# Two blocks on one core: the seam from the last feed-forward panel to the second block's first panel, met tile by tile

## The reference

```
block 1: x += mixed(rmsnorm(x) @ w_in) @ w_o            # differential attention and retention
         x += cross_attention(rmsnorm(x), rmsnorm(mem)) @ w_xo
         x += (silu(hf @ w_gate) * (hf @ w_up)) @ w_down,  hf = rmsnorm(x);  D_FF = 5632
         x  = rmsnorm(x) * norm_f_g
block 2: h  = rmsnorm(x) * pre_g * (1 + scale) + shift   # scale, shift from silu(c) @ w_ada + b_ada
         q, k, v, gate_a, u, gate_p = split(h @ w_in_2)
         windowed attention and pooling, gated, merged through w_merge, then w_out, a norm and the residual
```

## Time and profile before

| what | value |
|---|---|
| median of 3 runs | 2111.03 us |
| profiled execution's own time | 2107.38 us |
| its span | 2105.6 us |
| granted TensorE clock, mean | 0.998 |
| PE busy | 2062.9 us (98%) |
| VectorE busy | 1678.6 us (80%) |
| ScalarE busy | 1174.8 us (56%) |
| GpSimd busy | 72.9 us (3%) |
| moved by DMA | 453.75 MB, mean 215 GB/s |

### The profile page before, as it was taken

How to read it: one execution, slowest core, us unless ns; L and a number is a source line. 1 busy time by engine, 2 the same in 40 slices (tenths; PEclk the granted TensorE clock), 3 DMA queues, 4 the chain that set the end, 5 groups by cost and what they waited for, 6 DMA issues and landing times.

```text
span 2105.6 us, 25372 instructions
## 1 busy us (share of the span) xinstructions
PE 2062.9 (98%) x9334; PEld 1697.2 (81%) x9334; DVE 1678.6 (80%) x1839; ACT 1174.8 (56%) x1519; POOL 72.9 (3%) x94
## 2 busy tenths in 40 slices
PE   9999999999999999999999999999899999999998
PEld 7877888788887888888888888888678888888786
DVE  6777778876766788998889888898688768988875
ACT  6665656755554565554555555555556645554453
POOL 1000000000000000000000000000310000000000
PEclk9999999999999999999999999999999999999999
DMA  9555557565543458777777777675465556789752
GB/s 341 162 178 167 179 173 245 198 202 191 187 162 131 160 190 285 251 260 252 237 239 258 259 242 248 234 273 204 131 201 180 180 190 221 269 289 319 230 196 105
DMA packets 218955, 453.75 MB, mean 215 GB/s; under 512 B 14400, under 2 KB 16592, under 8 KB 218704
## 3 DMA queue, kind: packets, MB, share of 16 engines
q1 hardware_dynamic: 212928, 432.07, 61.0%
q0 software_dynamic: 5616, 19.94, 3.0%
q10 hardware_dynamic: 288, 0.13, 0.0%
HBM read 447.88 MB, written 4.19 MB: 215 GB/s over the span
## 4 chain that ended last, share of the span: by engine, by line
PE 83%; issue 7%; DVE 6%; ACT 3%; DMA 1%; POOL 0%; DVEq 0%; ACTq 0%; POOLq 0%
PE ps L1068 26%; PE ps L1070 26%; PE ps L1069 26%; DVE wlo L2311 2%; PE ps L648 2%; ACT whi L1587 1%; PE ps L798 1%; PE ps L778 1%; DVE raw L2324 0%; ACT junk L1099 0%; PE ps L884 0%; PE ps L926 0%; PE ps L915 0%; PE ps L864 0%; DMA FR<-in_mem_dram 0%
## 5 line engine op out<-in xcount | busy, mean ns | idle before, releaser
L2311 DVE TENSOR_TENSOR wlo<-raw,whi 128x1024 fp32r<-128x1024 f32 x832 | 1006.5, 1221 | 261.1 <-ACT whi L1587 255.0
L1587 ACT ACTIVATE whi<-raw 128x1024 fp32r<-128x1024 f32 x840 | 882.4, 1057 | 592.5 <-PE ps L1070 551.4
L1068 PE MATMUL ps<-whi,ah 128*128 128x512 f32 x1618 | 642.9, 397 | 13.6 <-DVE wlo L2311 5.5
L1070 PE MATMUL ps<-whi,al 128*128 128x512 f32 x1618 | 631.6, 390 | 0.0
L1069 PE MATMUL ps<-wlo,ah 128*128 128x512 f32 x1618 | 630.5, 390 | 0.0
L1068 PEld LDWEIGHTS ps<-whi,ah 128*128 128x128 f32 x1618 | 304.2, 188 | 80.1 <-issue 8.3
L1070 PEld LDWEIGHTS ps<-whi,al 128*128 128x128 f32 x1618 | 304.1, 188 | 64.7
L1069 PEld LDWEIGHTS ps<-wlo,ah 128*128 128x128 f32 x1618 | 304.5, 188 | 61.0 <-issue 0.2
L1068 PE MATMUL ps<-whi,bh 128*128 128x512 f32 x862 | 341.2, 396 | 3.5 <-DVE wlo L2311 3.1
L1070 PE MATMUL ps<-whi,bl 128*128 128x512 f32 x862 | 336.1, 390 | 0.0
L1069 PE MATMUL ps<-wlo,bh 128*128 128x512 f32 x862 | 335.6, 389 | 0.0
(11 more groups left out here) (235 smaller groups left out, 1335.6 us busy)
## 6 DMA issues: line engine op xcount, KB each, us to landing
raw<-in_w_in_dram SPq DMA_DIRECT2D x168, 512.0 KB, 4.5
raw<-in_w_ada_dram SPq DMA_DIRECT2D x96, 512.0 KB, 4.6
raw<-in_w_gate_dram SPq DMA_DIRECT2D x88, 512.0 KB, 4.8
raw<-in_w_up_dram SPq DMA_DIRECT2D x88, 512.0 KB, 5.0
raw<-in_w_down_dram SPq DMA_DIRECT2D x88, 512.0 KB, 5.4
raw<-in_w_merge_dram SPq DMA_DIRECT2D x64, 512.0 KB, 4.9
raw<-in_w_o_dram SPq DMA_DIRECT2D x32, 512.0 KB, 4.7
raw<-in_w_xk_dram SPq DMA_DIRECT2D x32, 512.0 KB, 4.6
```

Of the source, the lines that this page charges most:

```text
L1068: e.matmul(o, xh[:, k, tokens], wh, start=first, stop=False, skip_group_check=more)
L1070: ins = e.matmul(o, xl[:, k, tokens], wh, start=False, skip_group_check=more, stop=kk == 1 and (st.end or st.form in READ))
L1587: done(e.activation(whi[:, n % HALVES, :], place(item), ACT.Copy), "hi")
L2311: done(e.tensor_tensor(wlo[:, n % HALVES, :], src, whi[:, n % HALVES, :].bitcast(F32), ALU.subtract), "lo")
```

## The change

- e3 and kv meet six halves tile by tile instead of four: e3 all its six, kv its first six.
- The first two halves of e3 are split into `ah` and `al` (places of chunks 2 and 3), the first two of kv into the buffers of the forms; the ring of 4 goes on with the others. `_slots` works out for every half where it lies, from when that is free, and at which step it is made (for single-tile steps no more than 4, in kv 3, steps ahead of its use).
- The low parts of kv are made by VectorE like all others; GpSimd makes none.
- The pieces alternate between two pairs of banks, T and A, and their order is (0,0), (1,0), (2,0), (0,1), (1,1), (2,1), (3,1), (3,0).
- The work at the end of e3 is cut up: `down_sum`, `down_gain`, `down_mean` on VectorE, `down_square`, `gain_square` on ScalarE; and `modulated` into `mod_sums` and `mod_high` or `mod_low`. A job `second_input` orders them by step. Tile 1's sum comes at the end of e3, ahead of chunk 0's low part for tile 0.

```diff
@@ Stream
-        made = self._done + HALVES
...
+        for h, at in {("e", 3): ((0, ("a", 2)), (1, ("a", 3))),
+                      ("kv", 0): ((0, "forms_a"), (1, "forms_b"))}.get((panel.kind, panel.i), ()):
+            self.aside_at[base + h] = at
+        by_tile = HALVES + sum(base <= m for m in self.aside_at)
+        a, b = {"first": (0, by_tile), "last": (n - by_tile, n), None: (n, n)}[panel.stagger]
...
+    def _slots(self):
+        self.slot, self.slot_free, ring = {}, {}, []
+        for n in range(self.total):
+            if n in self.aside_at:
+                self.slot[n], self.slot_free[n] = self.aside_at[n], self.free[n]
+            else:
+                self.slot[n] = len(ring) % HALVES
+                self.slot_free[n] = ring[-HALVES] + 1 if len(ring) >= HALVES else 0
+                ring.append(n)
...
+        met = made = 0
+        for i, st in enumerate(self.steps):
+            ahead = len(self.steps)
+            if len(st.tiles) == 1 and st.form is None:
+                ahead = 3 if self.panels[st.p].stagger == "first" else HALVES
+            while made < self.total and self.slot_free[made] <= met and (
+                    made in self.aside_at or first_use[made] <= i + ahead):
+                made += 1
+            self.steps[i] = st._replace(made=made)
+            if st.taken:
+                met = st.n + 1
@@ PE
-                    jobs.start(pause(2))
-                    for j, tt in (first_order, second_order)[t]:
-                        jobs.start(modulated(j, tt))
-                    if t == 1:
+                    if t == 0:
+                        jobs.start(pause(4))
+                        for j, tt in mod_order:
+                            jobs.start(modulated(j, tt))
+                            if (j, tt) in ((1, 0), (2, 0)):
+                                jobs.start(pause(1))
+                    else:
                         jobs.start(make_forms())
                         jobs.start(first_result())
@@ ScalarE
+            def second_input():
+                yield from pause(4)
+                mod_sums(0, 0)
+                mod_high(0, 0)
+                yield
+                yield
+                mod_sums(1, 0)
+                gain_square(1)
+                mod_high(1, 0)
+                yield
+                yield
+                scale_chunk(1, 1)
+                mod_sums(2, 0)
+                mod_high(2, 0)
+                yield
+                for i, (j, t) in enumerate(mod_order[3:]):
+                    for nj, nt in mod_order[5 + i:6 + i]:
+                        if nj % 2:
+                            scale_chunk(nj, nt)
+                    mod_sums(j, t)
+                    mod_high(j, t)
+                    yield
@@ VectorE
+            def second_input(p):
+                yield from pause(4)
+                scale_chunk(2, 0)
+                mod_sums(0, 0)
+                yield
+                yield
+                mod_low(0, 0)
+                down_gain(p, 1)
+                mod_sums(1, 0)
+                yield
+                down_mean(1)
+                mod_low(1, 0)
+                yield
+                scale_chunk(0, 1)
+                mod_sums(2, 0)
+                mod_low(2, 0)
+                yield
...
                 elif kind == "e":
-                    last_down(p, t)
+                    down_sum(p, t)
+                    if t == 0:
+                        down_gain(p, t)
+                        down_mean(t)
+                        scale_chunk(0, t)
+                        jobs.start(second_input(p))
+                    else:
+                        jobs.start(make_forms("mod"))
+                        jobs.start(first_result())
@@ make, VectorE
-                    if n in stream.pool_halves:
-                        continue
-                    src = place(stream.entries[n].item)
+                    hi, lo = split_at(n)
                     e.wait_ge(s["hi"], n + 1)
@@ GpSimd
             final_roots(0)
-            low_parts(4)
             final_roots(1)
-            low_parts(8)
```

More of the change, by code:

```diff
@@ L267, in __init__ @@
         self._places()
+        self._slots()
         self._loads()
@@ L287, in _step @@
               aside=None):
-        made = self._done + HALVES
-        self.steps.append(Step(n, p, c, hf, tiles, form, start, end, made, job, taken, snap, aside))
-        if taken:
-            self._done = n + 1
+        self.steps.append(Step(n, p, c, hf, tiles, form, start, end, None, job, taken, snap, aside))
         if end:
@@ L594, in hs_done, with mod_banks @@
         def hs_done(j, t):
-            return s[f"hs{j % 2}"], 2 * (j // 2) + t + 1
+            own = [c for c in mod_order if c[0] % 2 == j % 2]
+            return s[f"hs{j % 2}"], own.index((j, t)) + 1
+        def mod_banks(j, t):
+            return A if mod_order.index((j, t)) % 2 else T
         def tmp_before(j, t):
@@ L611, in hi_lo, with split_at @@
             return [buf[:, 4 * c:4 * c + 4, :] for buf in at[name]]
+        def split_at(n):
+            at_n = stream.slot[n]
+            if isinstance(at_n, int):
+                return whi[:, at_n, :], wlo[:, at_n, :]
+            if isinstance(at_n, tuple):
+                parts = [buf[:, 4 * at_n[1]:4 * at_n[1] + 4, :] for buf in at[at_n[0]]]
+            else:
+                parts = [buf[:, :, :] for buf in forms[at_n[-1]]]
+            return [part.rearrange("p a b -> p (a b)") for part in parts]
         def two(ap, b):
@@ L832, in modulated @@
                 e.wait_ge(*hs_done(j, t))
-                for b in range(2):
-                    take(T[b], f"mod{j}{t}")
+                banks = mod_banks(j, t)
+                for bank in banks:
+                    take(bank, f"mod{j}{t}")
                 for k in range(4):
-                    ins = e.transpose(T[k // 2].ap[:, (k % 2) * P:(k % 2 + 1) * P],
+                    ins = e.transpose(banks[k // 2].ap[:, (k % 2) * P:(k % 2 + 1) * P],
                                       hs_of(j, t)[:, k * P:(k + 1) * P], ident[:, :])
                     if k % 2:
-                        ins.then_inc(T[k // 2].full, 1)
+                        ins.then_inc(banks[k // 2].full, 1)
                 yield
@@ L1608, in scalar_program @@
                     jobs.step()
-                if st.end and panels[st.p].stagger == "last" and i + 1 < len(stream.steps):
+                if st.end and panels[st.p].kind == "out" and panels[st.p].stagger and i + 1 < len(stream.steps):
                     make(stream.steps[i + 1].made)
@@ L2040, in last_down, with mod_sums @@
                 done(e.tensor_scalar(col, col, 1.0 / D, None, ALU.mult), "ms")
[L2041 to L2057, removed]
+            def mod_sums(j, t):
+                tmp, bank, label = tmp_of(j, t), mod_banks(j, t)[1], f"mod{j}{t}"
+                e.wait_ge(bank.full, bank.n(label))
                 before = tmp_before(j, t)
@@ L2359, in pool_program @@
             e.memset(ones[:, :], 1.0).then_inc(s["ones"], 1)
-            made = [0]
             def root(name, of, src, dst):
```

124 lines of the change are left out of this document (58 added, 66 removed).

## The result

| | before | after |
|---|---|---|
| median of 6 runs | 2110.22 us (2108.13 to 2111.13) | 2103.86 us (2102.03 to 2105.48) |
| profiled execution, its span | 2107.38, 2105.6 us | 2103.96, 2102.1 us |
| seam: e3's first matmul to the pair's first normal step | 58.77 us | 53.86 us |

The ratio after to before is 0.9972, 95% interval 0.9960 to 0.9985: 0.28% faster, 3 to 8 us. The forecast was 2106.3, 4.7 us less than the kernel before; the medians of six runs differ by 6.4.

The account below looks back on a forecast made before the run. TensorE, busy 98%, bounds the kernel; only 14.1 us of seam waits can be won. Seam 54.4 against 58.8 gives 4.4 less, with a later 0.3 wait 4.7 less, off 2111.0: 2106.3 us; 8-in-10 range 2100.5 to 2111.0.

Parts of the forecast that it names:

- timetable: Each engine's queue in the seam rebuilt from the new order, e3's first matmul = 0: 54.4 us against 58.8.
- the wait of 0.33 in the pair: Later wait in the pair, at 1550.84 on a low part; should go, 0.3 us, since result products now precede the pair.
- First chunk: kv's first half: PE starts at 20.7 after waiting 3.4 us, the fourth half's low part preceding tile 1's sum.
- Second chunk: kv's third half: PE ready at 23.9, starts at 26.7, a 2.8 us wait behind the fifth half's low part.
- Third chunk: Tile 0's third chunk in kv: PE ready at 29.9, starts at 30.3, a wait of 0.4 us.
- Tile 1's chunks: Tile 1's five chunks in kv: low parts done 32.7 to 41.0, no wait; before, waits cost over 4 us.
- the banks' gain: Second pair of banks lets PE turn a chunk before the last is read; gain counted within tile 1's chunk times.
- End of kv: Seventh half at 45.2 after a 2.1 us wait; pair's third step at 54.4 after waiting 0.9.
- Low parts moved: Eight low parts from GpSimd add 9.8 us to VectorE; 7.5 of stretch returns; its total goes from 41.6 to some 44.
- Rival 1: Cover works better than the queues say: only chains count in the seam, 10 us less, 2101; chance 0.2.
- Rival 2: Gain lost again in the pair through VectorE's queue: 1.7 us less is left, 2109.3; chance 0.22.
- Rival 3: VectorE becomes the bound as the stretch stays: 7.6 us later, 2.9 slower than before, 2113.9; chance 0.08.

Follow-up runs that it names:

- experiment 10: Changed kernel with kv's third and fourth half split one step earlier in e3; seam 53.97 us.
- experiment 6: Changed kernel with tile 1's sum behind chunk 0's low part instead of ahead of it; seam 56.39 us.
- experiment 7: experiment 6's kernel with PE kept busy in its three waits by 13, 9 and 9 matmuls of ones; seam 54.47 us.
- experiment 4: Changed kernel with all eight pieces turned into one pair of banks, T; seam 53.89 us.
- experiment 5: experiment 1's kernel with two pairs of banks, order of the pieces kept; seam 58.87 us.
- experiment 1: Kernel before with only kv's low parts moved from GpSimd to VectorE; seam 58.85 us.
- experiment 11: experiment 10's kernel with kv's fifth and sixth half also split one step later; seam 51.56 us, median 2099.95 us, ratio to before 0.9962.
- experiment 12: experiment 11's kernel with the pair's forms two job steps later; seam 49.41 us, median 2099.98 us, ratio to before 0.9956.
- experiment 9: Changed kernel without halves in idle buffers, four halves by tile for six, pause two steps for four; seam 65.03 us.
- experiment 8: experiment 1's kernel with 12 matmuls of ones ahead of chunk 1's transposes; seam 60.25 us.
- experiment 2: Changed kernel with kv's low parts back on GpSimd; seam 55.84 us.
- experiment 3: experiment 2's kernel with PE kept busy by 14 and 8 matmuls of ones in two waits; seam 55.58 us.

## Why the prediction was right

- **The number.** 2103.86 lies within the range for 8 in 10 (2100.5 to 2111.0) and just under the forecast's own (2104.5 to 2108.0); as a difference, 6.4 us is just inside its 3 to 6.5. The timetable accounts for 5.2 of it (below).
- **Where.** All that could be won was placed in the seam, as 14.1 us of waits. Of the 58.77 us the change took 4.91, and the wait of 0.33 in the pair went as said. From e3's first matmul to the end the profiled executions took 2105.6 - 1481.4 = 624.2 and 2102.1 - 1483.7 = 618.4 us, 5.8 less.
- **First chunk.** Predicted at 20.7, measured 1504.22 - 1483.71 = 20.5. The waiting low part of kv's fourth half in front of the sum is in VectorE's rows and in experiment 10.
- **Second chunk.** Predicted at 26.7, measured 26.2; but the wait was 0.6, not 2.8: PE was late itself, with 8 matmuls at half clock, and that filled the wait. The clock was not in my timetable. It cost nothing here, because what PE lost it would have waited; experiments 6 and 7 have this step at 26.8 with such a fall and without. That the end of the seam came out to 0.5 us all the same is in this a piece of luck: a fall behind the wait at kv's seventh half, as experiment 6 had it, cost 0.7 there.
- **Third chunk.** 0.4 predicted, none seen. **Tile 1's chunks.** No wait, as said. That the banks' gain "is in these" was empty: experiments 4 and 5 give it nothing.
- **End of kv.** Seventh half predicted at 45.2, measured 44.7; the pair's step at 54.4, measured 53.9. Waits 1.8 and 0.7 for 2.1 and 0.9.
- **Low parts moved.** I had 7.5 us of stretch back against 9.8 of work: VectorE's sum went from 41.6 to 40.5 where I had 44. The sum was mis-sized at both ends: with e3's first two low parts made ahead of the seam only six more fall in it (12 for 6), not eight, and three of the chunks' own low parts had been stretched too, to 1.19, 1.00 and 1.31 us against 0.69. The exchange is worth 1.7 us in the new order and nothing in the old, which I had overrated (experiment 1). The Trainium skill's rule (SBUF — State Buffer, "Who interferes with whom") agrees with the trace: with GpSimd reading SBUF the gain product took 2.15 to 2.89, without 0.68 to 0.69. In the kernel before it started at 1504.41 and ended 0.5 us after the low part that GpSimd ran from 1503.18 to 1506.02, as a block for the whole length would have it.
- **Rival 1** (only the chains count) was wrong for the change itself, and describes what experiments 11 and 12 reach by moving the splits out of the way: first wait 1.32 for its 1.3, none at the second and third chunk. **Rival 2** didn't come: the pair's wait was 0.74. **Rival 3**: nothing stayed stretched.
- The seam and pair explain 5.2 us or a little more; the runs say 3 to 8. The rest of 6.4 is within what the runs spread by.

## What to carry to other kernels

Where the engines run one written order, rebuild each queue instruction by instruction around the wait: here that gave every wait to 0.5 us but for the clock, while sums of work per engine said little. The same working was wrong by 10 us where I misread one queue (experiment 9), so it is worth a check against the rows. Ask for each wait what stands in front of the late instruction that it doesn't need; moving four splits by one step and one job by two took 4.4 us more from the seam, after a rewrite that had taken 4.9 (0.9 of it came back in the pair). A part that gives nothing in the old order (low parts on VectorE) may give in a new one, so undo parts from the new kernel, not only add them to the old.

## What the runs showed of the hardware that I had not expected

- The granted clock fell to 0.50, for 3.4 us at a time (6.8 in experiments 1, 5 and 8, 10.2 in 9), at waits of PE in this seam: at 3.11 (the changed kernel and experiment 4), 2.67 (experiment 2), 3.17 (5), 3.57 (8), 9.21 and 2.26 (9), 2.51, 1.83 and 1.87 (experiment 6), 2.18 and 1.89 (experiment 10), 2.98 (experiment 11); not at 2.63 in the kernel before, 2.19 in experiment 5, 2.04 in 9, 1.80 in the changed kernel, nor 1.3 and less in experiment 12. So the length of the wait alone doesn't tell. Filling the waits with matmuls kept it at 1.00 in experiments 3 and 7, and in experiment 7 made the seam 1.9 us shorter with more work; in experiment 8 the fall came at the next wait. A fall cost where PE was then the one waited for (0.3 us in experiment 2, 1.2 and 0.7 in 6), and nothing where another wait followed (the first in 6, and the one in 1).
- It also falls far ahead of the seam, differently from execution to execution of kernels that are the same there. Windows of experiment 3 and of experiment 7, the stretch 160 to 180 us:

```profile
160.00:180.00 20.00, 17.95 (x83) 14.42 (x82) 15.39 (x27) 12.70 (x30) 0.69 (x1) 1.00 0.49 158
```

```profile
160.00:180.00 20.00, 17.94 (x75) 14.26 (x74) 14.45 (x27) 9.79 (x21) 0.69 (x1) 0.91 0.46 146
```

  The first had no fall before e3 and reached it at 1479.8 us, the second three and reached it at 1484.9; those with one (experiments 4, 6, 9 and 11) reached it at 1481.2 to 1481.7. That is as much as the whole change, so a single execution's total can't judge it. The seam's own length is free of these falls, though not of those inside it.
